# Two later head groups of dilated attention, taken by residue mod 4 with their own softmax

## The chip, the cores and the metric

One core of one Trainium2 chip. The metric is the device time of one execution in microseconds (us). TensorE is called PE, VectorE DVE, ScalarE ACT, GpSimd POOL and SyncE SP.

## What is computed

One layer of a decoder with three mixers on the same normalised input: a gated convolution, stick-breaking attention and dilated windowed softmax attention, merged by gates, then an MLP. It runs for a prompt of 512 tokens and for 8 sequences of one new token each (520 columns in all). The change is in the dilated attention of the prompt: three groups of four heads of 64 channels, with (window, dilation) of (128, 1), (512, 4) and (2048, 16). The groups' outputs are weighted by their softmax denominators, which is one softmax over the keys of all three groups:

```python
DIL_GROUPS = ((128, 1), (512, 4), (2048, 16))
...
    logits = jnp.einsum('nbqhd,nbkhd->nbhqk', qs, kb).astype(jnp.float32) * (HEAD_DIM ** -0.5) + bias
    logits = jnp.where(valid[None, :, None], logits, -jnp.inf)
    lse = jax.nn.logsumexp(logits, axis=-1)
    p = jnp.exp(logits - lse[..., None])
    o = jnp.einsum('nbhqk,nbkhd->nbqhd', p.astype(v.dtype), vb)
...
def combine_groups(outs, lses, dtype):
    w = jax.nn.softmax(jnp.stack(lses, axis=0), axis=0)
    o = jnp.sum(w[..., None] * jnp.stack(outs, axis=0).astype(jnp.float32), axis=0)
```

A query of group 1 sees only keys at a distance that is a multiple of 4, one of group 2 only multiples of 16.

## The kernel before

Every weight of the layer is streamed once, in units of 128 output channels. A unit is loaded by SP (`wraw`, three slots), split by ACT into a high part (`whi`) and by POOL or DVE into the rest (`wlo`). PE then works through **ticks**: a tick is one half (260 columns) of one unit, 24 matmuls (8 slices of the input, 3 products each: `whi` by `xh`, `whi` by `xl`, `wlo` by `xh`) into a PSUM bank of the ring G0, G1, G2. There are 324 ticks. DVE takes each result (`take`), so a bank is used again three ticks later. Units come in this order: sq, sk, sv (ticks 0 to 23), dq, dk, dv (24 to 59, six tiles each), four times cc, ch, cb (60 to 83), gates g0, g1, g2 (84 to 107), and from tick 108 the branches, out, up and down. After the second half of a `ch` tile DVE runs `convolve`, six instructions over `convu` and `convy` (ticks 63, 69, 75, 81).

Everything else is laid between the ticks by `make_plan`: a table of stages by half tick. Every engine walks the same table in order and runs its part of each stage, so an entry sets the order on all engines. A stage at an even entry stands in the middle of a tick for PE (after 12 of the 24 matmuls), one at an odd entry at the tick's end; on DVE and ACT the odd ones come after the take and after the `whi` split. Around the change stand `p_*` (stick-breaking attention of the prompt, ticks 20 to 59), `dv_rows` (transposes of dv), `v_sum` (one page step of the sampled sequences, four pages of 256 KB loaded by SP), `s_*` (dilated attention of the sampled sequences) and `branch_split` (ACT and DVE split the finished branches, `convy`, `o_sbT`, `o_dT`, into high and low parts).

The dilated attention of the prompt runs from tick 61 to tick 101. A work item w is a pair of heads `jp` (0, 1; e is the head in the pair) and a block `i` of 128 queries. Its stages: `l_scores` for each group g, queries of block i by the keys, in token order: the last 256 of them for group 0, and all keys up to the block's end for groups 1 and 2, 128 (i + 1) columns, in which `bias` masks what the dilation leaves out (by a value of -1e30). The scores go to the banks S0 (e = 0) and S1 (e = 1), one each; DVE scales them and adds the bias into `lg`, and after the third group takes the maximum over all 384 to 1280 columns (`lmax`). `l_weights`: ACT's exponential in place, with the row sum in `stat`. `l_turn`: PE transposes the blocks of one head and one group to the bank TR, ACT copies them to `lT`. `l_sum`: PE sums the values by them into the bank OU. At the end of each pair of heads `l_out` copies OU to `o_dT`, `l_root` turns the reciprocals `rsum` of the row sums, and `l_mul` spreads them over 64 rows each and multiplies. The bank TR is shared with `dv_rows`, `s_turn`, `s_vd`, `v_red` and `p_turn`; OU with `p_sum`. A bank is opened on PE by a wait until the engine that read its last contents is done. An fp32 matmul shows in the trace as two instructions.

## Time and profile before

| | |
|---|---|
| median of 3 runs | 1104.13 us (1103.65 to 1106.02) |
| the profiled execution | 1104.08 us |
| its span in the trace | 1102.3 us |
| PE busy | 1050.9 us, 95% |
| DVE, ACT, POOL busy | 41%, 38%, 28% |
| DMA | 211.08 MB, 191 GB/s on average |

The span runs from the first instruction to the last. Busy time of PE is counted from a matmul's start to its modelled end, and neighbours overlap, so 95% doesn't mean a PE at its peak: what a matmul costs is read from the distance of one start to the next. Start times in the views are microseconds from the span's start.

### The profile page before, as it was taken

What the parts mean: (1) busy time and instruction counts of PE and PEld (TensorE: products, weight loads), DVE (VectorE), ACT (ScalarE), POOL (GpSimd) and SP (SyncE); (2) the same over time, 40 slices, a digit from 0 to 9 for tenths busy, and PEclk for the clock granted to TensorE, in tenths of its full rate; (3) what the DMA queues carried; (4) which work ended last, traced back from release to release, by engine and by line L of the source; (5) the groups of instructions that cost most, each with busy time, mean ns of one, the idle gap of its engine ahead of it and who ended that gap; (6) DMA issues with size and microseconds to landing.
All of it is one profiled execution on the core that took longest, in us unless ns stands there. A gap on an engine that the chain in (4) does not pass through costs nothing.

```text
span 1102.3 us, 21957 instructions
## 1 busy us (share of the span) xinstructions
PE 1050.9 (95%) x8694; PEld 947.8 (86%) x8694; DVE 453.5 (41%) x805; ACT 422.0 (38%) x730; POOL 310.7 (28%) x141
## 2 busy tenths in 40 slices
PE   6999999998999989999999999989999999999995
PEld 6886778876778667778999999989999999999995
DVE  5313455775145523333543476743113212212434
ACT  5214556674233222334333323454134224313534
POOL 2422232211222220001212122224443444334620
PEclk9999999999999998999999999999999999999998
DMA  7588887774885575511422325736557367467202
GB/s 270 181 271 300 288 249 232 262 238 153 291 279 197 174 267 178 187 58 40 174 96 88 100 82 190 283 111 248 207 203 272 137 243 284 145 258 267 77 1 78
DMA packets 65945, 211.08 MB, mean 191 GB/s; under 512 B 7850, under 2 KB 10155, under 8 KB 63667
## 3 DMA queue, kind: packets, MB, share of 16 engines
q1 hardware_dynamic: 65842, 209.67, 55.2%
q8 instruction: 70, 1.15, 0.4%
q14 instruction: 33, 0.26, 0.1%
HBM read 202.16 MB, written 51.48 MB: 230 GB/s over the span
## 4 chain that ended last, share of the span: by engine, by line
PE 83%; DVE 5%; ACT 4%; issue 3%; DMA 2%; SPq 1%; POOL 1%; DVEq 0%; ACTq 0%
PE G L1284 52%; PE S L1284 14%; PE Z L1284 11%; PE TR L1287 3%; PE OU L1284 2%; DMA wraw<-in_w_in_dram 2%; ACT whi L681 1%; POOL wlo L653 1%; DVE convy L958 1%; SPq L543 1%; SPq L544 1%; ACT lg L824 0%; DVE mtmp L958 0%; DVE macc L955 0%; DVE pw L1149 0%
## 5 line engine op out<-in xcount | busy, mean ns | idle before, releaser
L1284 PE MATMUL G<-xh,whi 128*128 128x260 f32 x1288 | 380.3, 295 | 14.2 <-DVE xl L958 9.8
L1284 PE MATMUL G<-xl,whi 128*128 128x260 f32 x1288 | 366.8, 285 | 0.0
L1284 PE MATMUL G<-xh,wlo 128*128 128x260 f32 x1288 | 366.1, 284 | 0.0
L653 POOL TENSOR_TENSOR wlo<-wraw,whi 128x1024 fp32r<-128x1024 f32 x61 | 149.1, 2444 | 533.1 <-ACT whi L681 533.1
L1284 PEld LDWEIGHTS G<-xh,whi 128*128 128x128 f32 x1288 | 246.0, 191 | 44.2 <-issue 29.5
L1284 PEld LDWEIGHTS G<-xl,whi 128*128 128x128 f32 x1288 | 245.9, 191 | 0.0
L1284 PEld LDWEIGHTS G<-xh,wlo 128*128 128x128 f32 x1288 | 245.4, 191 | 0.0
L653 POOL TENSOR_TENSOR wlo<-mraw,whi 128x1024 fp32r<-128x1024 f32 x56 | 135.2, 2415 | 201.6 <-ACT whi L681 201.5
L681 ACT ACTIVATE whi<-wraw 128x1024 fp32r<-128x1024 f32 x83 | 87.9, 1059 | 221.8 <-PE G L1284 185.1
L681 ACT ACTIVATE whi<-mraw 128x1024 fp32r<-128x1024 f32 x56 | 59.4, 1061 | 157.3 <-PE G L1284 54.9
L955 DVE TENSOR_TENSOR tg<-G,rstd 128x260 f32<-128x260 f32 x48 | 20.4, 427 | 85.1 <-PE G L1284 85.0
L1284 PE MATMUL G<-hidh,whi 128*128 128x260 f32 x192 | 54.3, 283 | 0.0
L1284 PE MATMUL G<-hidh,wlo 128*128 128x260 f32 x192 | 54.2, 282 | 0.0
L1284 PE MATMUL G<-hidl,whi 128*128 128x260 f32 x192 | 54.1, 282 | 0.0
L1284 PE MATMUL S<-xh,whi 128*128 128x260 f32 x176 | 50.5, 287 | 2.9 <-DVE xl L955 2.9
L955 DVE TENSOR_TENSOR hT<-hT,G 128x260 f32<-128x260 f32 x47 | 19.9, 423 | 77.2 <-PE G L1284 77.2
L1284 PE MATMUL S<-xl,whi 128*128 128x260 f32 x176 | 50.2, 285 | 0.0
L1284 PE MATMUL S<-xh,wlo 128*128 128x260 f32 x176 | 50.1, 285 | 0.0
L1284 PE MATMUL G<-binh,whi 128*128 128x260 f32 x160 | 45.7, 285 | 1.3 <-issue 1.3
L955 DVE TENSOR_TENSOR hidl<-msq,hidh 128x260 fp32r<-128x260 f32 x64 | 44.7, 699 | 4.8 <-ACT hidh L681 4.8
L900 ACT ACTIVATE msq<-mt 128x260 f32<-128x260 f32 x64 | 26.5, 414 | 52.4 <-DVE mt L958 52.4
L1284 PE MATMUL G<-binh,wlo 128*128 128x260 f32 x160 | 45.2, 283 | 0.0
(261 smaller groups left out, 2090.3 us busy)
## 6 DMA issues: line engine op xcount, KB each, us to landing
wraw<-in_w_in_dram SPq DMA_DIRECT2D x66, 512.0 KB, 5.0
kv<-in_kpool_dram SPq DMA_DIRECT2D x128, 256.0 KB, 3.3
kv<-in_vpool_dram SPq DMA_DIRECT2D x128, 256.0 KB, 3.4
mraw<-in_w_up_dram SPq DMA_DIRECT2D x32, 512.0 KB, 3.5
mraw<-in_w_down_dram SPq DMA_DIRECT2D x32, 512.0 KB, 3.5
out_win_k_kept_dram<-in_cache_win_k_dram SPq DMA_DIRECT2D x8, 2047.0 KB, 9.1
out_win_v_kept_dram<-in_cache_win_v_dram SPq DMA_DIRECT2D x8, 2047.0 KB, 10.5
wraw<-in_w_ab_dram SPq DMA_DIRECT2D x8, 512.0 KB, 3.4
```

The costliest lines, as they stand in the source:

```text
L543: page = sp.value_load(pages[0:1, idx:idx + 1], min_val=0, max_val=x["kpool"].shape[0] - 1)
L544: sp.dma_start(kv[:, slot, 512 * p:512 * p + 512], x["kpool"][bass.ds(page, 1)].rearrange("a p c -> (a p) c")).then_inc(kv_in[slot], 16)
L653: nc.gpsimd.tensor_tensor(low(u), raw(u)[0], high(u).bitcast(F32), ALU.subtract).then_inc(w_lo, 1)
L681: return nc.scalar.activation(out, in_, ACT.Copy, **kw)
L900: nc.scalar.activation(msq[:, h], mt[:, h], ACT.Square).then_inc(m_sq, 1)
L955: return nc.vector.tensor_tensor(out, a, b, op)
L958: return nc.vector.scalar_tensor_tensor(out, a, scalar, b, op0, op1)
L1284: return nc.tensor.matmul(out, lhsT, rhs, start=start, stop=stop, **kw)
L1287: return nc.tensor.transpose(out, in_, ident[0:rows, 0:rows])
```

## The change

- dq, dk and dv of tiles 2 to 5 (groups 1 and 2) are stored in residue order: token 4p + r at column 128 r + p of the first 512. DVE's take writes them so, with a stride; the take of the second half becomes two instructions, since the 8 columns of the sampled tokens stay where they are. The host turns the stored dk and dv back.
- A query of residue r meets in groups 1 and 2 only keys of residue r. A step is now `(jp, sub, i)`: sub 0 is group 0, one block of queries by two blocks of keys (one for i = 0) as before; sub 1 is groups 1 and 2 together, i is the residue, and each of the two groups has one block of 128 keys. There are 16 steps (`LSTEPS`) of at most 256 columns for each head.
- The two subs have their own maximum and sum (`lstat`), their own OU contents and outputs (`o_dT`, `o_sub`). They are joined at the end: `l_stat` turns maxima and sums into rows, DVE and ACT (`l_power`) make from them a share for each sub (`share`), and `l_mul` spreads the shares, multiplies both outputs and adds them.
- `lg` is a ring of four steps instead of one item; both heads of a step are transposed in one `l_turn` of up to four blocks, and `lT` has two halves that steps use in turn. `bias` is loaded once, 1 MB, instead of four loads of 640 KB.
- One step stands at each whole tick from 61 on: scores of step m at tick 61 + m, weights a tick later, transposes two, sums three. All are odd entries. `v_sum` is rounded to the same entries. The join is at ticks 78 to 82, `branch_split` at 96 and 97 (before at 100 and 101). `s_turn` and `s_vd` move to 64 and 65.

The diff, cut; of the stage functions of DVE, ACT and PE (in this order, behind the take) only what stands there now, since the lines that they replace are printed above.

```diff
-BW = 1280
+BW = 512
 ...
-    for w in range(DLI):
-        jp, i = w // QB, w % QB
-        t = l0 + 4.5 * w + 1.5 * jp
-        if i == 0:
-            add(l0 - 3 if jp == 0 else t - 1.5, "bias_load", jp)
-        for g in range(NG):
-            add(t + 0.5 * g, "l_scores", NG * w + g)
-        add(t + 1.5, "l_weights", w)
-        for g in range(NG):
-            add(t + 2.5 + g, "l_turn", 6 * w + 2 * g)
-            add(t + 3 + g, "l_turn", 6 * w + 2 * g + 1)
-            add(t + 3.5 + g, "l_sum", NG * w + g)
-        if i == QB - 1:
-            add(t + 5.5, "l_out", jp)
-            add(t + 3.5, "l_root", jp)
-            add(t + 6, "l_mul", jp)
-    l_end = t + 6
+    add(l0 - 3, "bias_load")
+    for m in range(LSTEPS):
+        add(l0 + m, "l_scores", m)
+        add(l0 + m + 1, "l_weights", m)
+        add(l0 + m + 3, "l_sum", m)
+        if m % QB == QB - 1:
+            add(l0 + m + 3, "l_out", m // QB)
+        add(l0 + m + 2, "l_turn", m)
+    t = l0 + LSTEPS
+    add(t + 1, "l_stat", 0)
+    add(t + 2, "l_power")
+    add(t + 2, "l_stat", 1)
+    add(t + 4, "l_mul", 0)
+    add(t + 5, "l_mul", 1)
+    l_end = max(t + 6, v_end + 6, at("cb", 3) + 2)
 ...
-                    tt(plain[kind][:, tile, half(h)], src, root, ALU.mult).then_inc(dve_took, 1)
+                    if kind in ("dq", "dk", "dv") and tile >= 2:
+                        n = HALF if h == 0 else S - HALF
+                        dst = by_residue(plain[kind][:, tile, 0:S])[:, h * HALF // 4:(h * HALF + n) // 4, :]
+                        rows = [in_order(a[:, 0:n]) for a in (src, root)]
+                        if h == 0:
+                            tt(dst, *rows, ALU.mult).then_inc(dve_took, 1)
+                        else:
+                            link(tt(dst, *rows, ALU.mult))
+                            tt(plain[kind][:, tile, S:TOK], src[:, n:HALF], root[:, n:HALF], ALU.mult).then_inc(dve_took, 1)
+                    else:
+                        tt(plain[kind][:, tile, half(h)], src, root, ALU.mult).then_inc(dve_took, 1)
 ...
             def l_scores(m):
+                jp, sub, i, blocks = l_step(m)
+                n, end = P * blocks, BW if sub else 256
                 if m == 0:
                     await_bank(dve, "p_sum", QB - 1)
+                    dve.wait_ge(bias_in, 16)
+                if m >= LRING:
+                    await_bank(dve, "l_turn", m - LRING)
+                logits = lg[:, m % LRING, :, 0:n]
                 for e in range(2):
                     src = await_bank(dve, "l_scores", m, e)
+                    stt(logits[:, e, :], src[:, 0:n], SCALE, bias[:, 2 * jp + e, end - n:end],
                         ALU.mult, ALU.add).then_inc(of(read, "l_scores", m, e), 1)
+                for e in range(2):
+                    await_taken(dve, "l_scores", m, e)
+                nc.vector.tensor_reduce(lstat[:, 0, sub, i, 2 * jp:2 * jp + 2], logits, AX.X, ALU.max,
+                                        negate=True).then_inc(l_made, 1)
+            def l_stat(kind):
+                own, sub, both = share[0:GH, 0, :], share[0:GH, 1, :], share[0:GH, 0:2, :]
+                low, more = share[0:GH, 2, :], share[0:GH, 3, :]
+                srcs = [await_bank(dve, "l_stat", kind, n)[0:GH, :] for n in range(2)]
+                if kind == 0:
+                    await_bank(dve, "l_turn", LSTEPS - 1)
+                    nc.vector.tensor_copy(own, srcs[0]).then_inc(of(read, "l_stat", 0, 0), 1)
+                    nc.vector.tensor_copy(in_order(sub), by_residue(srcs[1])).then_inc(of(read, "l_stat", 0, 1), 1)
+                    for n in range(2):
+                        await_taken(dve, "l_stat", 0, n)
+                    link(tt(low, own, sub, ALU.min))
+                    tt(both, low.unsqueeze(1).to_broadcast([GH, 2, S]), both, ALU.subtract).then_inc(l_less, 1)
+                else:
+                    dve.wait_ge(l_power, 1)
+                    tt(low, srcs[0], own, ALU.mult).then_inc(of(read, "l_stat", 1, 0), 1)
+                    tt(in_order(more), by_residue(srcs[1]), in_order(sub), ALU.mult).then_inc(of(read, "l_stat", 1, 1), 1)
+                    for n in range(2):
+                        await_taken(dve, "l_stat", 1, n)
+                    link(tt(low, low, more, ALU.add))
+                    link(nc.vector.reciprocal(low, low))
+                    tt(both, both, low.unsqueeze(1).to_broadcast([GH, 2, S]), ALU.mult).then_inc(l_share_made, 1)
             def l_mul(jp):
+                parts = (o_dT[:, jp, 0:S], o_sub[:, jp, :])
+                for sub in range(2):
+                    await_taken(dve, "l_sum", 2 * jp + sub)
+                    src = await_bank(dve, "l_mul", jp, sub)
+                    tt(parts[sub], parts[sub], src[:, :], ALU.mult).then_inc(of(read, "l_mul", jp, sub), 1)
+                for sub in range(2):
+                    await_taken(dve, "l_mul", jp, sub)
+                tt(parts[0], parts[0], parts[1], ALU.add).then_inc(l_done, 1)
 ...
+            def l_weights(m):
+                jp, sub, i, blocks = l_step(m)
+                act.wait_ge(l_made, m + 1)
                 for e in range(2):
+                    col = 2 * jp + e
+                    logits = lg[:, m % LRING, e, 0:P * blocks]
+                    nc.scalar.activation(logits, logits, ACT.Exp, bias=lstat[:, 0, sub, i, col:col + 1],
+                                         accum_out=lstat[:, 1, sub, i, col:col + 1]).then_inc(l_pmade, 1)
             def l_turn(m):
+                cols = 2 * P * l_step(m)[3]
+                copy(lT[:, m % 2, 0:cols], await_bank(act, "l_turn", m)[:, 0:cols]).then_inc(read["TR"], 1)
+            def l_out(n):
+                jp, sub = n // 2, n % 2
+                src = await_bank(act, "l_sum", n)
+                if sub:
+                    copy(in_order(o_sub[:, jp, :]), by_residue(src[:, :])).then_inc(read["OU"], 1)
+                else:
+                    copy(o_dT[:, jp, 0:S], src[:, :]).then_inc(read["OU"], 1)
+            def l_powers(_):
+                act.wait_ge(l_less, 1)
+                nc.scalar.activation(share[0:GH, 0:2, :], share[0:GH, 0:2, :], ACT.Exp).then_inc(l_power, 1)
 ...
             def l_scores(m):
+                jp, sub, i, blocks = l_step(m)
                 if m == 0:
                     pe.wait_ge(dve_took, at("dk", 5) + 1)
                 dst = [open_bank(pe, "l_scores", m, e) for e in range(2)]
+                queries = slice(P * i, P * i + P)
+                keys = queries if sub else slice(P * (i + 1 - blocks), P * i + P)
+                for n in range(2 if sub else 1):
+                    for e in range(2):
+                        t, rows = head(GH * (sub + n) + 2 * jp + e)
+                        out = dst[e][:, P * n:P * n + P] if sub else dst[e][:, 0:P * blocks]
+                        ins = mm(out, dqT[rows, t, queries], dkT[rows, t, keys], True, True)
+                        if n == sub:
+                            ins.then_inc(of(written, "l_scores", m, e), 1)
+            def l_turn(m):
+                blocks = l_step(m)[3]
+                pe.wait_ge(l_pmade, 2 * m + 2)
+                dst = open_bank(pe, "l_turn", m)
                 for e in range(2):
+                    for b in range(blocks):
+                        c = P * (blocks * e + b)
+                        ins = turn(dst[:, c:c + P], lg[:, m % LRING, e, P * b:P * b + P])
                 ins.then_inc(written["TR"], 1)
             def l_sum(m):
+                jp, sub, i, blocks = l_step(m)
+                if m == 0:
+                    for n in range(2 * NG):
+                        await_taken(pe, "dv_rows", n)
+                if m % QB == 0:
+                    open_bank(pe, "l_sum", m // QB)
+                await_taken(pe, "l_turn", m)
+                for b in range(blocks):
+                    g, rows = (1 + b, i) if sub else (0, i + 1 - blocks + b)
                     for e in range(2):
                         d0 = 256 * g + HD * (2 * jp + e)
+                        c = P * (blocks * e + b)
+                        ins = mm(bank["OU"][HD * e:HD * e + HD, P * i:P * i + P], dv_tok[:, rows, d0:d0 + HD],
+                                 lT[:, m % 2, c:c + P], b == 0, b == blocks - 1, tile_position=(0, HD * e))
+                if m % QB == QB - 1:
                     ins.then_inc(written["OU"], 1)
+            def l_stat(kind):
+                if kind == 0:
+                    pe.wait_ge(l_made, LSTEPS)
+                else:
+                    pe.wait_ge(l_pmade, 2 * LSTEPS)
+                for sub in range(2):
+                    dst = open_bank(pe, "l_stat", kind, sub)
+                    for i in range(QB):
+                        ins = turn(dst[0:GH, P * i:P * i + P], lstat[:, kind, sub, i, :])
+                    ins.then_inc(of(written, "l_stat", kind, sub), 1)
             def l_mul(jp):
+                pe.wait_ge(l_share_made, 1)
+                for sub in range(2):
+                    dst = open_bank(pe, "l_mul", jp, sub)
+                    for e in range(2):
+                        col = 2 * jp + e
+                        ins = mm(dst[HD * e:HD * e + HD, :], ident[0:GH, col:col + 1].to_broadcast([GH, HD]),
+                                 share[0:GH, sub, :], True, True, tile_position=(0, HD * e))
+                    ins.then_inc(of(written, "l_mul", jp, sub), 1)
```

In what follows, `S<-dkT,dqT` are the scores, `TR<-ident,lg` transposes, `OU<-lT,dv_tok` value sums, `Z<-kv,wT` a page sum and `G<-xh,whi` the projection.

PE around tick 75, whose first half is done when the first row comes; this is before, with one group's scores in the middle of the tick and another group's at its end:

```order
L1284 MATMUL OU<-lT,dv_tok 64x128 [waits read_TR]
L1284 MATMUL OU<-lT,dv_tok 64x128 x5
L1287 MATMUL TR<-ident,lg 128x128 [waits read_TR,l_pmade]
L1287 MATMUL TR<-ident,lg 128x128 x2
L1284 MATMUL S<-dkT,dqT 128x256 [waits read_S1,read_S0]
L1284 MATMUL S<-dkT,dqT 128x256
L1284 MATMUL G<-xh,whi 128x260
```

And with the change, the end of tick 75, after 24 projection matmuls in a row:

```order
L1320 MATMUL Z<-kv,wT 32x512 [waits kv_in1]
L1320 MATMUL Z<-kv,wT 32x512 x3
L1320 MATMUL OU<-lT,dv_tok 64x128 [waits read_TR]
L1320 MATMUL OU<-lT,dv_tok 64x128 x3
L1323 MATMUL TR<-ident,lg 128x128 [waits read_TR,l_pmade]
L1323 MATMUL TR<-ident,lg 128x128 x3
L1320 MATMUL S<-dkT,dqT 128x128 [waits read_S1,read_S0]
L1320 MATMUL S<-dkT,dqT 128x128 x3
```

Each request for the score banks moves to the end of a tick, with everything else of the step ahead of it.

DVE at the same place, before: `convolve` of tick 75, then the reads of both groups' scores and two maxima.

```order
L1133 TENSOR_SCALAR convy<-convu,cvec 128x520 [waits dve_done]
L958 SCALAR_TENSOR_TENSOR convy<-convu,cvec,convy 128x512 [waits dve_done] x2
L958 SCALAR_TENSOR_TENSOR convy<-cvec,convy 128x8 [waits dve_done]
L1137 COPY utail<-convu 128x10 [waits dve_done]
L958 SCALAR_TENSOR_TENSOR convy<-cvec,convy 128x8 [waits dve_done]
L958 SCALAR_TENSOR_TENSOR lg<-S,bias 128x512 [waits written_S0,bias_in]
L958 SCALAR_TENSOR_TENSOR lg<-S,bias 128x512 [waits written_S1]
```

And with the change, DVE at tick 75 and the first rows of tick 76:

```order
L962 SCALAR_TENSOR_TENSOR convy<-cvec,convy 128x8 [waits dve_done]
L962 SCALAR_TENSOR_TENSOR lg<-S,bias 128x256 [waits written_S0,written_TR]
L962 SCALAR_TENSOR_TENSOR lg<-S,bias 128x256 [waits written_S1]
L1190 TENSOR_REDUCE lstat<-lg 128x2 [waits read_S1,read_S0]
L959 TENSOR_TENSOR convy<-convy,G 128x260 [waits made,conv_made]
```

Behind the convolution DVE now reads one step of 256 columns for each head and takes one maximum for both, then comes the next take. The join on DVE, at ticks 78 and 79 (the middle row is the take of tick 79):

```order
L1199 COPY share<-S 4x512 [waits written_TR,written_S1,written_S0]
L1200 COPY share<-S 4x512
L959 TENSOR_TENSOR share<-share 4x512 [waits read_S1,read_S0]
L959 TENSOR_TENSOR share<-share 4x1024 [waits dve_done]
L959 TENSOR_TENSOR convu<-G,rstd 128x260 [waits made]
L959 TENSOR_TENSOR share<-S,share 4x512 [waits l_power,written_S1,written_S0]
L959 TENSOR_TENSOR share<-S,share 4x512
L959 TENSOR_TENSOR share<-share 4x512 [waits read_S1,read_S0]
L1212 RECIPROCAL share<-share 4x512 [waits dve_done]
L959 TENSOR_TENSOR share<-share 4x1024 [waits dve_done]
```

It is new; the takes of ticks 79 to 81 stand between and behind its parts.

## Rows read from the trace of the kernel before

**Rows 1.** The page, engines: busy us, share of the span, instructions.
```profile
PE 1050.9 (95%) x8694; PEld 947.8 (86%) x8694; DVE 453.5 (41%) x805; ACT 422.0 (38%) x730; POOL 310.7 (28%) x141
```

**Rows 2.** Chain of waits in order of time: start us, us, what.
```profile
539.24 107.19 PE G L1284 x894
```

**Rows 3.** Busy time by stretch: stretch, its us, PE, PEld, DVE, ACT, POOL, clock, DMA share, GB/s.
```profile
289.14:524.70 235.56, 223.74 (x1805) 172.42 (x1803) 92.51 (x165) 77.55 (x137) 42.23 (x17) 0.98 0.55 184
372.00:380.00 8.00, 5.80 (x37) 3.56 (x36) 5.93 (x11) 0.41 (x1) 0.00 (x0) 0.79 0.54 161
409.00:421.00 12.00, 7.72 (x41) 5.41 (x41) 7.07 (x14) 1.31 (x4) 2.50 (x1) 0.72 0.26 89
...
296.60:302.10 5.50, 5.50 (x45) 4.17 (x44) 1.41 (x5) 1.66 (x2) 2.38 (x1) 1.00 1.00 375
```

**Rows 4.** PE's waits in 289.14:524.7: waiting <- releaser: total us, times, longest us.
```profile
PE S L1284 <- DVE lg L958: 6.5, 2, 4.3
PE TR L1287 <- ACT lT L681: 1.6, 2, 0.8
PE TR L1287 <- ACT o_dT L681: 1.2, 1, 1.2
```

**Rows 5.** Groups of PE instructions in 289.14:524.7: count | busy us, mean ns | idle before.
```profile
L1287 PE MATMUL TR<-ident,lg 128*128 128x128 f32 x108 | 21.3, 288 | 2.4 <-ACT o_dT L681 1.2 <-ACT o_sbT L681 0.6 <-ACT vd L681 0.6
L1284 PE MATMUL S<-dkT,dqT 64*128 64x256 f32 (+3 forms) x96 | 19.1, 475 | 6.5 <-DVE lg L958 6.5
L1284 PE MATMUL OU<-lT,dv_tok 128*64 128x128 f32 x216 | 17.1, 284 | 0.6 <-ACT lT L681 0.6
```

**Rows 6.** Timeline of PE, six places: start us, us, instruction, count.
```profile
336.64 0.66 PE L1284 MATMUL OU<-lT,dv_tok 128*64 128x128 f32 x8
337.23 0.44 PE L1287 MATMUL TR<-ident,lg 128*128 128x128 f32 x2
337.43 0.37 PE L1284 MATMUL G<-xh,whi 128*128 128x260 f32 x1
337.63 0.28 PE L1284 MATMUL G<-xl,whi 128*128 128x260 f32 x1
...
369.32 1.13 PE L1284 MATMUL S<-dkT,dqT 64*128 64x512 f32 x4
370.38 0.39 PE L1284 MATMUL G<-xh,whi 128*128 128x260 f32 x1
...
392.86 0.66 PE L1287 MATMUL TR<-ident,lg 128*128 128x128 f32 x4
393.28 0.37 PE L1284 MATMUL G<-xh,whi 128*128 128x260 f32 x1
...
404.64 1.07 PE L1284 MATMUL TR<-rT,ident 2*64 2x512 f32 x4
405.65 0.49 PE L1284 MATMUL S<-dkT,dqT 64*128 64x128 f32 x4
406.07 0.39 PE L1284 MATMUL G<-xh,whi 128*128 128x260 f32 x1
```

**Rows 7.** Timeline of DVE at tick 75: start us, us, instruction, count.
```profile
368.03 0.43 DVE L955 TENSOR_TENSOR convu<-convu,G 128x260 f32<-128x260 f32 x1 [0.86 <-PE G L1284]
...
369.48 3.53 DVE L958 SCALAR_TENSOR_TENSOR convy<-convu,cvec,convy 128x512 f32<-128x512 f32 x2
...
373.66 1.28 DVE L958 SCALAR_TENSOR_TENSOR lg<-S,bias 128x512 f32<-128x512 f32 x2
```

**Rows 8.** Groups of ACT and DVE by shape: count | busy us, mean ns.
```profile
L681 ACT ACTIVATE qz<-sqT 64x32 f32<-64x32 f32 x2 | 0.5, 256 | 0.0
L681 ACT ACTIVATE dvs<-dvT 128x48 f32<-128x48 f32 x1 | 0.2, 225 | 0.0
...
L1183 DVE RECIPROCAL rsum<-stat 128x8 f32<-128x8 f32 x2 | 0.4, 193 | 0.0
L1219 DVE RECIPROCAL scol<-scol 128x1 f32<-128x1 f32 x1 | 0.2, 152 | 0.0
```

**Rows 9.** PE's waits in 240:289: waiting <- releaser: total us, times, longest.
```profile
PE TR L1287 <- DVE pT L1158: 5.3, 4, 2.6
```

More of the change, by code:

```diff
@@ L1503, in l_scores @@
             def l_scores(m):
-                w, g = m // NG, m % NG
-                jp, i = w // QB, w % QB
-                full, first, _ = n_keys(i)
+                jp, sub, i, blocks = l_step(m)
                 if m == 0:
                     pe.wait_ge(dve_took, at("dk", 5) + 1)
-                k0 = full - first if g == 0 else 0
                 dst = [open_bank(pe, "l_scores", m, e) for e in range(2)]
-                for e in range(2):
-                    t, rows = head(GH * g + 2 * jp + e)
-                    mm(dst[e][:, 0:full - k0], dqT[rows, t, P * i:P * i + P], dkT[rows, t, k0:full], True,
-                       True).then_inc(of(written, "l_scores", m, e), 1)
@@ L1602, in prompt_bias @@
 def prompt_bias(rel_bias):
[L1604 to L1608 removed]
+    out = np.full((P, GH, BW), MASK, np.float32)
+    row, col = np.arange(P)[:, None], np.arange(P)[None, :]
+    near = P + row - np.arange(2 * P)[None, :]
+    for g, c, dist in ((0, 0, near), (1, 2 * P, 4 * (row - col)), (2, 3 * P, 4 * (row - col))):
+        dil = DIL[g][1]
         ok = (dist >= 0) & (dist % dil == 0) & (dist // dil <= P)
@@ L1611, in prompt_bias @@
         for j in range(GH):
-            out[j, :, col:col + width] = np.where(ok, rel_bias[b, GH * g + j], np.float32(MASK))
-        col += width
+            out[:, j, c:c + dist.shape[1]] = np.where(ok, rel_bias[b, GH * g + j], np.float32(MASK))
     return out
```

155 lines of the change are left out of this document (43 added, 112 removed).

## Prediction

> **What bounds the kernel now.** I read the page's busy line first: TensorE (PE) is busy 95% of the span, and no other engine reaches half of it [rows 1]. Then the chain of waits in order of time: late in the kernel it runs through 894 projection matmuls in a row, 107.19 us, or 0.120 us each [rows 2]. A tick is 24 of them, 2.88 us, and the kernel has 324 ticks. So time can only be gained where PE does something other than projections, where it waits, or where its clock is low. Then the stretch that the change touches, from the start of tick 60 to the start of tick 104 (289.14 to 524.70): 235.6 us for 44 ticks that alone would take 44 x 2.88 = 126.7. The other 109 us are what stands between the projections. DMA is busy 55% of it, at 184 GB/s, VectorE (DVE) 39% [rows 3], so neither is the bound on average. The last view is who PE waited for in it [rows 4]. The waits are few but dear: two of them, on DVE's `lg`, cost 6.5 us.
>
> **Matmul work removed.** The counts are 96, 108 and 216 instructions for scores, transposes and value sums [rows 5]; an fp32 matmul shows as two, so these are 24 pairs of heads for scores, 108 transposed blocks, and 24 runs of sums. Prices are the distance from one start to the next in the timeline [rows 6]. Scores of one head pair: 0.42 us for 128 keys (405.65 to 406.07), 1.06 for 512 (369.32 to 370.38); in between I draw a line, 0.63 for 256 and 0.85 for 384. Before: 6 pairs of 128 keys, 10 of 256, 4 of 384, 4 of 512: 2.5 + 6.3 + 3.4 + 4.2 = 16.4 us. After: 18 pairs of 128 and 6 of 256: 7.6 + 3.8 = 11.4. Transposes: 0.20 us for a run of 2, 0.42 for 4, so about 0.3 for 3 and 0.09 for 1. Before 12, 20, 8 and 8 runs of 1, 2, 3 and 4 blocks: 1.1 + 4.0 + 2.4 + 3.4 = 10.9; after 2 runs of 2 and 14 of 4: 6.3. Value sums: a run of 8 instructions takes 0.59 (336.64 to 337.23), a run of 12 follows the same slope; I use 0.37, 0.59, 0.81 and 1.03 for 4, 8, 12, 16. Before 6, 10, 4, 4 of these: 2.2 + 5.9 + 3.2 + 4.1 = 15.4; after 2 and 14: 9.0. The joining: before 2 runs of four small transposes (0.4) and 2 spreads over 64 rows (1.01, 404.64 to 405.65), 2.8 us; after 4 and 4 of them, 5.6. In all 45.5 before, 32.3 after: **-13.2 us**, all of it on PE and so on the path.
>
> **Fewer interruptions.** After other work, the first projection matmul lasts 0.20 instead of 0.12 us (337.43 to 337.63) [rows 6], and the last one before it is drawn out about as much: 0.16 us an interruption. By the plan, PE leaves the projection at 73 half ticks of this stretch before, and at 39 after, since a step now stands whole at a tick's end. 34 x 0.16 = **-5.4 us**.
>
> **Waits removed.** The two `lg` waits come from DVE's order. At the last tick of each `ch` tile DVE takes the bank and convolves: it begins at 368.03 and gets to `lg` at 373.66, 5.6 us later [rows 7]. The score banks S0 and S1 are single. Before, PE asks for them again half a tick later and stands; after, a whole tick later: 2.88 us of projection, a page sum (1.0), value sums (0.6) and transposes (0.4) behind the first request, and 2.0 us of the same kind before that projection. That is some 7 us against 5.6 + 1.3 for DVE. It just fits, so I let the 6.5 us go. The two waits on `lT` before `rsum` (1.6) and the one on `o_dT` (1.2) go with the code that has them [rows 4]: 9.3 in all. The clock goes with them: granted 0.79 of full over 372:380 and 0.72 over 409:421 [rows 3], the two places of the `lg` waits. At 1.2 instead of 2.4 GHz that is 3.4 and 6.7 us at half speed, half of it lost: 5.1 us. Together **-14.4 us**. What is late next is nothing on PE: the next step's scores have their bank a tick ahead.
>
> **What it adds.** (a) Takes of dq, dk and dv for tiles 2 to 5 now write with a stride of 128 elements, and those of the second half are two linked instructions. The trace has no strided DVE write. ScalarE (ACT) has one: `qz`, 32 scattered elements, 256 ns, against `dvs`, 48 in runs of 8, 225 ns [rows 8]: about 1.4 ns an element more than its own contiguous rate. From that, a take costs 0 to 0.36 us more, and 0.2 more where it is split. DVE is not PE's bound there; but four waits on `pT` (5.3 us) stand in 240:289 [rows 9], and a take lies in front of the longest. Bounds 0 and 3 us; I take 1.0. (b) The join on DVE after step 15: two copies, minimum, subtraction, then after ACT's exponential two products, a sum, a reciprocal of 4x512, a product. 8 elements of reciprocal take 193 ns and one 152 [rows 8], so 512 take some 3 us; the rest are instructions of 0.7 to 1.2 us. The chain is about 13 us from the start of tick 79, and PE wants the result at the end of tick 81, 2.9 + 2 x 4 + 2 = 13 us later. A wait of 0 to 4 us; I take 0.7. Queued behind it on DVE are takes 80 and 81, which PE needs three ticks later: hidden. (c) `branch_split` now stands at ticks 96 and 97, in ticks of 2.88 us without any cover: its 1.9, 1.9 and 1.1 us on ACT delay `whi`. It was so before too; +1.0. (d) The supply of V pages, below: +0.5. One load of the bias of 1 MB takes the place of four of 640 KB, a gain where nobody waits: nothing. Sum **+3.2 us**.
>
> At (a) the Trainium skill speaks against the change: the page SBUF — State Buffer, section Door 1: The DMA port swizzle, says in its note on cachelines that an access that crosses to a new 16-byte line pays a penalty, so fp32 may stride 4 elements for free. It gives no price. If every element paid one more DVE cycle, the 24 takes would grow by 0.27 us each; no row here shows it for DVE.
>
> **The sum.** -13.2 - 5.4 - 14.4 + 3.2 = -29.8 us. The profiled run took 1104.08 us with a span of 1102.3, and the median of the runs is 1104.13, so nothing has to be corrected: **1074 us**.
>
> **Rivals.**
> 1. *The convolution still holds the banks, or the join comes late.* The fit above is about 7 against 6.9 us. If it fails at the three ticks 63, 69 and 75 and at the join by 1 to 2 us each, PE stands 4 to 7 us and the clock falls once or twice (1.7 us each, as at 372:380): +7, 1081 us. For it: DVE's two long convolution instructions take 3.53 us [rows 7], and what feeds the steps between (ACT's exponentials) follows them. Against: DVE's own work of a step is shorter than before, two reads of 256 columns and one maximum.
> 2. *The pages become the bound.* From tick 78 on only page sums stand between the projections: 1.15 ticks at 2.88 and one sum, 4.5 us for 1.05 MB of pages and 0.30 MB of weights, 300 GB/s. In 296.60:302.10 the queues moved 375 GB/s with DMA full [rows 3], so it fits; if 285 GB/s were the limit, 0.25 us for each of 11 sums, and a wait with a drop of the clock behind it: +5, 1079 us.
> 3. *Strided takes are dear.* DVE is loaded in ticks 28 to 59. At twice the ACT surcharge, 0.7 us a take, its waits on `pT` grow and ACT is late behind it: +6 to +10, 1082 us.
> 4. *Slower than before, the same place, by another price:* 24 strided takes in 24 ticks. PE may reuse a G bank three ticks later, so a take hides until DVE itself is full. In ticks 40 to 59 DVE has about 1.2 us free a tick. Beyond that, each us of a take is a us of PE: from 2.5 us more a take (5 times 0.42, 10 ns an element) the 24 takes cost 24 x 1.3 = 31 us and the gain is gone; at 3 us it would be 24 x 1.8 = 43, 1117 us. Only if each element took ten cycles.
> 5. *It doesn't do what it says:* the stretch is not bound by PE. Its 95% and the 13.2 us of matmul speak against; 1104 us.
>
> **How the numbers follow.** The forecast (1068 to 1079) has 0.60, rivals 1 and 2 together 0.20 (1077 to 1087), rival 3 0.09, rival 4 0.03, rival 5 0.02. In 0.06 it is better than 1068: all added costs hidden, 1104.1 - 33.0 = 1071, and the short waits on `vd`, `o_sbT` and `lT` that I left uncounted gone too. The range 1066 to 1086 leaves out rivals 4 and 5, the dear end of rivals 1 and 3, and what lies beyond 1066: 0.16. Faster by over 0.2% (2.2 us, about what a measurement of this kernel can tell): 0.95; within 0.2%: 0.02; slower: 0.03.
>
> **What would show it.** In the profile after: S<-dkT, TR<-ident,lg and OU<-lT with 96, 60 and 120 instructions; ticks 61 to 77 of about 5.7 us each; no wait of PE for `lg` over 1 us and a granted clock of 1.00 from tick 61 to tick 104; the stretch of ticks 60 to 103 at 204 to 207 us. Takes `dqT<-G` with shape 65x4 at 0.42 to 0.8 us. Wrong: PE waits for `lg` at ticks 64, 70, 76; `kv` pages among PE's releasers; takes over 1 us.

## The result, and the profile after

The changed kernel takes **1071.55 us** (median of 4 runs, 1069.96 to 1073.68), the kernel before 1103.98 (1103.65 to 1106.02). The ratio is 0.971, with a 95% interval of 0.967 to 0.974: 32.4 us less, where 1074 us and 30 us less were forecast. The profiled run took 1069.96 us with a span of 1067.9.

The page of after, busy us of each engine; beside [rows 1] PE gives up 23 us (its weight loads, PEld, 13), and no other engine moves by more than 10:

```profile
PE 1027.5 (96%) x8566; PEld 934.8 (88%) x8566; DVE 458.4 (43%) x812; ACT 412.2 (39%) x731; POOL 311.2 (29%) x141
```

Busy time by stretch (stretch, its us, PE, PEld, DVE, ACT, POOL, clock, DMA share, GB/s): first ticks 60 to 103, which answer to 289.14:524.70 in [rows 3], then the place of the join:

```profile
287.65:490.38 202.73, 200.45 (x1676) 160.10 (x1675) 92.71 (x162) 68.06 (x139) 42.16 (x17) 1.00 0.62 203
...
400.00:418.00 18.00, 16.54 (x117) 10.60 (x116) 16.23 (x23) 2.00 (x2) 2.37 (x1) 1.00 0.68 209
```

The stretch fell from 235.6 to 202.7 us, by 32.8, and the clock is 1.00 all through it. DMA moves 203 instead of 184 GB/s. All of PE's waits in it, beside [rows 4]:

```profile
PE S L1320 <- DVE o_dT L959: 0.9, 1, 0.9
PE G L1320 <- POOL wlo L651: 0.8, 1, 0.8
PE S L1320 <- DVE share L959: 0.5, 1, 0.5
```

No wait for `lg` is left. Two short ones for the join are new. The groups that answer to [rows 5] (count | busy us, mean ns | idle before):

```profile
L1320 PE MATMUL OU<-lT,dv_tok 128*64 128x128 f32 x120 | 10.1, 286 | 0.0
L1323 PE MATMUL TR<-ident,lg 128*128 128x128 f32 x60 | 10.1, 288 | 0.0
L1320 PE MATMUL S<-dkT,dqT 64*128 64x128 f32 x72 | 6.7, 300 | 0.0
L1320 PE MATMUL S<-dkT,dqT 64*128 64x256 f32 x24 | 4.2, 428 | 0.0
```

Last, the block of other work at the end of tick 75, in PE's timeline (start us, us, instruction, count), and the start of the next block:

```profile
372.14 1.06 PE L1320 MATMUL Z<-kv,wT 128*32 128x512 f32 x8
373.14 0.66 PE L1320 MATMUL OU<-lT,dv_tok 128*64 128x128 f32 x8
373.73 0.66 PE L1323 MATMUL TR<-ident,lg 128*128 128x128 f32 x4
374.31 0.71 PE L1320 MATMUL S<-dkT,dqT 64*128 64x128 f32 x8
374.96 0.39 PE L1320 MATMUL G<-xh,whi 128*128 128x260 f32 x1
...
378.04 0.64 PE L1320 MATMUL Z<-kv,wT 128*32 128x512 f32 x4
```

A whole tick with a page sum and a softmax step is 378.04 - 372.14 = 5.90 us. Read the starts, not the durations, since those overlap: 1.00 for the page, 0.59 for value sums, 0.58 for transposes, 0.65 for scores, 3.08 for the projection. The prediction had 5.7. In what follows I add up such distances over ticks 60 to 103, each given to the instruction that starts it. Each column adds up to its stretch. A wait is in the instruction ahead of it, and the last row says how much of the column is waits.

```
us, ticks 60 to 103      before   e2      e1      after   e12
scores                    17.4    16.5     9.8     9.8     9.8
transposes of lg          13.7    13.7     5.7     8.7     6.2
value sums                17.7    15.4     9.0     9.0     9.0
joining                    2.7     2.7     5.3     5.3     5.3
projections              147.8   141.1   137.1   135.4   136.1
pages and the rest        36.2    35.3    36.5    34.6    33.7
stretch                  235.5   224.7   203.4   202.7   200.2
of it waits               11.9     5.4     3.2     2.2     1.3
```

Columns e2, e1 and e12 are experiments, below. Of the waits, 6.9, 2.6, 0.8, 1.3 and 1.3 us lie in the row of the projections, and 1.6 in that of the transposes before and in e2 (the two on `lT`).

### The profile page after: what moved, and what is told of

Same layout as the page of the kernel before. It is cut to its first block, busy times and chain, and to the rows that moved or that the text cites. A ratio compares the mean times of both kernels' runs of the same rounds, so it can differ in the third digit from the quotient of the medians.

```text
span 1067.9 us, 21643 instructions
## 1 busy us (share of the span) xinstructions
PE 1027.5 (96%) x8566; PEld 934.8 (88%) x8566; DVE 458.4 (43%) x812; ACT 412.2 (39%) x731; POOL 311.2 (29%) x141
## 4 chain that ended last, share of the span: by engine, by line
PE 87%; DVE 5%; ACT 3%; issue 2%; DMA 1%; POOL 1%; SPq 0%; DVEq 0%; ACTq 0%
PE G L1320 56%; PE S L1320 14%; PE Z L1320 12%; PE TR L1323 2%; PE OU L1320 2%; DMA wraw<-in_w_in_dram 1%; ACT whi L679 1%; POOL wlo L651 1%; DVE mtmp L962 0%; DVE macc L959 0%; DVE pw L1164 0%; DVE pT L1173 0%; DVE convu L959 0%; DVE share L1212 0%; PE TR L1320 0%
## 5 line engine op out<-in xcount | busy, mean ns | idle before, releaser
L1320 PE MATMUL G<-xh,whi 128*128 128x260 f32 x1288 | 375.5, 292 | 12.7 <-DVE xl L962 9.7
```

Of the source, the lines that this page charges most:

```text
L1320: return nc.tensor.matmul(out, lhsT, rhs, start=start, stop=stop, **kw)
```

## Experiments

### The waits alone

**e2_scores_first** is the kernel before, with the convolution moved behind the scores:

```
 elif kind == "ch":
     ...
-    if h:
-        convolve(tile)
 ...
+if k and TICKS[k - 1][1][0] == "ch" and TICKS[k - 1][2]:
+    convolve(TICKS[k - 1][1][4])
 take(k)
```

> The kernel before, with one edit on VectorE: the convolution of a tile runs after the read of the scores that PE sends in the next half ticks, instead of ahead of it. Matmul work and plan are as before. Theory: the two waits on lg (6.5 us) and the two falls of the clock behind them (5.1 us) go, 1104 - 11.6 = 1092.5 us (1091 to 1095), and the granted clock in 372:380 and 409:421 is 1.00. Rival A, the clock falls for another reason than the waits: only 6.5 us, 1097.5. Rival B, VectorE is late by as much somewhere else (a G bank, lT): 1102 to 1105.

Measured: 1092.85 us (1092.22 to 1094.93). Its stretch of ticks 60 to 103, and the two places at which the clock was 0.79 and 0.72 in [rows 3]:

```profile
287.39:512.14 224.75, 219.37 (x1804) 169.78 (x1803) 90.23 (x165) 77.56 (x137) 41.97 (x17) 1.00 0.58 193
372.00:380.00 8.00, 8.00 (x68) 6.42 (x66) 7.44 (x12) 4.18 (x6) 0.84 (x1) 1.00 0.70 212
405.00:421.00 16.00, 16.00 (x129) 12.14 (x128) 7.94 (x19) 6.78 (x14) 1.34 (x2) 1.00 0.74 233
```

DVE in it, at the same scores as [rows 7]:

```profile
368.84 1.29 DVE L958 SCALAR_TENSOR_TENSOR lg<-S,bias 128x512 f32<-128x512 f32 x2 [1.66 <-PE S L1284]
372.31 1.29 DVE L958 SCALAR_TENSOR_TENSOR lg<-S,bias 128x512 f32<-128x512 f32 x2 [2.19 <-PE S L1284]
...
376.82 1.54 DVE L958 SCALAR_TENSOR_TENSOR convy<-convu,cvec,convy 128x512 f32<-128x512 f32 x2
```

Now DVE waits for the scores, and PE no longer waits for DVE. With no matmul removed the stretch is 10.8 us shorter, where the theory gives 11.6 (6.5 of waits, 5.1 of clock). Rivals A (only the waits) and B (the wait moves) fall. The edit alone makes the kernel before 1% faster, and one third of the whole gain was two waits and what the clock made of them.

### Half ticks against whole ticks

**e1_half_ticks** is the kernel after with its work spread over both halves of a tick:

```
-        t = int(v0 + 1.15 * i + 1.5 * (i // PAGES))
+        t = v0 + 1.15 * i + 1.5 * (i // PAGES)
 ...
-        add(l0 + m + 3, "l_sum", m)
+        add(l0 + m + 4, "l_sum", m)
-        add(l0 + m + 2, "l_turn", m)
+        add(l0 + m + 2.5, "l_turn", m)
```

(`l_out` and the join follow a tick later.)

> The kernel after, with the same instructions spread over both halves of a tick: transposes a half tick later, value sums and the join a whole tick later, page sums at the half ticks they had before. Between the start of tick 60 and that of tick 104, PE then leaves the projection 55 times instead of 39. Theory, an interruption costs 0.16 us: the stretch grows from 202.7 by 2.6 us, to 205.3. Rival A, an interruption costs nothing on PE and only waits do: under 203.2. Rival B, the half tick between transposes and value sums is too short or DVE is asked too soon: waits of over 1 us, 206 or more.

Measured: 1071.27 us (1067.47 to 1075.32). The stretch, and its waits:

```profile
283.72:487.12 203.40, 200.09 (x1676) 160.29 (x1675) 92.37 (x162) 68.60 (x139) 42.25 (x17) 1.00 0.63 206
```

```profile
PE TR L1323 <- ACT spself L679: 1.0, 1, 1.0
PE S L1320 <- DVE share L959: 0.9, 1, 0.9
PE G L1320 <- POOL wlo L651: 0.8, 1, 0.8
PE TR L1323 <- ACT vd L679: 0.6, 1, 0.6
```

The stretch is 0.7 us longer than after's. It waits 3.2 us where after waits 2.2; without waits it is 200.2 against 200.5. So 16 more interruptions cost nothing in sum. That is rival A in substance, though its bound of 203.2 is missed by 0.2. But the table shows that an interruption has a price: without their waits the projections grow from 134.1 to 136.3 us, 0.14 for each of the 16. What makes up for it is that the transposes shrink by 3.0 us with the same 60 instructions. The transposes in e1's timeline, alone in the middle of a tick:

```profile
372.62 0.60 PE L1323 MATMUL TR<-ident,lg 128*128 128x128 f32 x4
372.98 0.37 PE L1320 MATMUL G<-xh,whi 128*128 128x260 f32 x1
```

Four transposes take 0.36 us here and 0.58 between value sums and scores. So their price depends on what stands beside them.

**e12_turns_last** tests that with the number of interruptions left at 39: the order inside the block becomes value sums, scores, transposes.

```
 for m in range(LSTEPS):
+    add(l0 + m + 3, "l_sum", m)
+    ...
+for m in range(LSTEPS):
     add(l0 + m, "l_scores", m)
+for m in range(LSTEPS):
     add(l0 + m + 1, "l_weights", m)
-    add(l0 + m + 3, "l_sum", m)
-    ...
     add(l0 + m + 2, "l_turn", m)
```

> The kernel after, with the order inside the block at the end of a tick changed on PE: value sums, scores, transposes, in place of value sums, transposes, scores. The count of interruptions stays at 39. Theory now: not leaving the projection has a price, but a change of kind between the small matmuls; a run of four transposes takes 0.587 us ahead of scores and 0.414 ahead of the projection, so the 15 ticks win 0.17 us each: -2.6 us in the stretch (202.7 to 200.1). Rival, the order is indifferent, and the first turn to another kind always costs the same: 202.7. Second rival, the scores ask for their banks 0.6 us sooner, behind the convolution of ticks 63, 69 and 75: a wait for lg of up to 0.5 us each.

Measured: 1069.97 us (1066.71 to 1070.82), against 1070.06 for after on the same chip. The medians can't tell 2.5 us apart, as the runs of one kernel lie 4 to 7 us apart there. The stretch can:

```profile
287.93:488.16 200.23, 198.88 (x1675) 160.75 (x1675) 92.62 (x162) 68.17 (x139) 42.16 (x17) 0.99 0.62 206
```

```profile
372.22 0.66 PE L1325 MATMUL TR<-ident,lg 128*128 128x128 f32 x4
372.63 0.37 PE L1322 MATMUL G<-xh,whi 128*128 128x260 f32 x1
```

200.2 us, 2.5 less than after, where 2.6 was expected; four transposes take 0.41 us, all of them together 2.5 us less, and there is no wait for `lg`. Both rivals fall. But two things that the expectation didn't have are in the 2.5. The granted clock fell to its lower level in the stretch, ahead of the last products of the join:

```profile
405.70:409.10 3.40, 3.40 (x19) 3.00 (x21) 3.19 (x8) 0.00 (x0) 0.00 (x0) 0.50 0.38 145
```

The matmuls there lose 1.6 us, and PE comes so late to the join that its wait of 0.9 us on `o_dT` in after is gone. That is 0.7 us net on the wrong side, so the agreement with 2.6 is partly luck, and at a level clock the order should be worth more than 2.5.

The block still changes its kind of matmul as often as in after. What has changed is the neighbour of the transposes, and by it the distances in the timelines fall into order. Transposes and projections use all 128 rows and columns of PE, page sums 32 columns, value sums 64 columns and scores 64 rows. Four transposes take 0.36 us between projections, 0.41 between a matmul of the smaller kinds and a projection, and 0.58 or 0.59 between a smaller one and scores. Page sums (1.00) and eight value sums (0.59) take the same whatever stands beside them. So it is the step from the transposes to smaller matmuls that costs, 0.17 us, and not each change of kind. The distances in before, e2, e1, after, e9 and e12 all fit this; it was read from them and not tested apart, and why it costs, no run shows.

**after_again** is the kernel after, run beside e12, e4 and e11:

> The kernel after, unchanged, to stand beside the other three on the same chip: 1071.5 us (1069.5 to 1074). By the trace, runs differ from each other only before tick 24 and in a fall of the clock near 250 us and 690 us.

Measured: 1070.06 us (1066.89 to 1073.48), ticks 60 to 103 in 202.6 us and ticks 24 to 59 in 186.08, against 202.7 and 186.06. Between these two runs such a stretch repeats within 0.1 us, with the clock up in both, and this is why stretches decide where medians don't.

### Is it PE's work that counts?

**e3_work_twice** issues every score matmul and every transpose twice:

```
-for n in range(2 if sub else 1):
+for n in (0, 1, 0, 1) if sub else (0, 0):
 ...
-for e in range(2):
+for e in (0, 1, 0, 1):
     for b in range(blocks):
         ...
         ins = turn(
```

> The kernel after, with every score matmul and every transpose of the later head groups issued twice into the same place; the result is the same. Theory, PE bounds the stretch, so work counts one for one: scores 2 x 0.42 + 6 x 0.63 + 8 x 0.645 = 9.8 us, transposes 6.3 us by the prediction's prices, +16.1 us on the kernel after (1071.5): 1087.6 (1085 to 1090). Rival, PE has slack in the stretch that the waits of other engines fill: +0 to +8, under 1080.

Measured: 1082.6 us (1080.66 to 1084.56). The stretch:

```profile
287.21:502.89 215.68, 213.40 (x1831) 172.78 (x1831) 92.74 (x162) 68.04 (x139) 42.05 (x17) 1.00 0.59 191
```

It grew by 13.0 us instead of 16.1, with the same waits as after; the median grew by 11.1 and lies below the range that was expected. That isn't slack. Added up from the timeline, the second run of eight scores takes 0.446 us instead of 0.645, of four transposes 0.436 instead of 0.587, of two pairs of 256 keys 0.431: 8 x 0.446 + 6 x 0.431 + 2 x 0.22 + 14 x 0.436 + 2 x 0.22 = 13.1. So work counts one for one, at the price of a run right behind its like. The size in the expectation was off, the mechanism is right.

### The strided takes

**e4_plain_takes** leaves out the reordering by residue (the edit makes `if kind in ("dq", "dk", "dv") and tile >= 2:` false).

> The kernel after with the takes of dq, dk and dv for tiles 2 to 5 written without the stride of 128 and in one instruction, so that the later head groups are computed on tokens in the wrong order; every instruction after the takes is as before. The prediction gave the strided takes +1.0 us (0 to 3): the kernel would be 1.0 us faster than after_again, all of it in ticks 24 to 59. Rival, a take is hidden behind the three ticks until its bank is asked for again: 0.0 to 0.2 us in ticks 24 to 59.

Measured: 1068.9 us (1065.38 to 1072.43) against 1070.06. The takes of dk, first in after, then in e4 (groups of DVE: count | busy us, mean ns):

```profile
L959 DVE TENSOR_TENSOR dkT<-G,rstd 128x260 f32<-128x260 f32 x8 | 4.2, 519 | 0.0
L959 DVE TENSOR_TENSOR dkT<-G,rstd 128x252 f32<-128x252 f32 x4 | 2.5, 616 | 0.0
L959 DVE TENSOR_TENSOR dkT<-G,rstd 128x8 f32<-128x8 f32 x4 | 0.7, 167 | 0.1
```

```profile
L959 DVE TENSOR_TENSOR dkT<-G,rstd 128x260 f32<-128x260 f32 x12 | 5.0, 420 | 0.0
```

Of the first group half are strided: 2 x 519 - 420 = 0.62 us against 0.42, so 0.20 more for 260 elements, and 0.36 more for the half that is two instructions. On PE nothing of it arrives: ticks 24 to 47 take 115.45 us in e4 and 115.46 in after_again. In ticks 48 to 53 e4 is even 1.3 us slower, because the clock fell at PE's longest wait on `pT` (2.6 us):

```profile
249.00:258.00 9.00, 6.57 (x40) 5.38 (x40) 5.12 (x11) 4.10 (x7) 1.92 (x1) 0.81 0.05 6
```

The profile of after has the same wait (2.8 us) without the fall, so this is one of the things that make runs of one kernel differ. The medians, 1.2 us apart, lie within the scatter of either kernel. The rival holds: 0.0 and not 1.0 us.

**e5_takes_3x** and **e6_takes_5x** issue the strided product three and five times (a loop of two and of four more around `link(tt(dst, *rows, ALU.mult))`).

> The kernel after, with the strided product in each of the 24 takes of dq, dk and dv for tiles 2 to 5 issued three times on VectorE: +1.24 us a take. Theory (rival 4 of the prediction): VectorE has about 1.2 us free a tick in ticks 40 to 59, so this hides but for the waits on pT: +0 to +4 us on 1071.5. Rival, VectorE is already on the path there and each us counts: 24 x 1.24 = +30, 1101.

> The kernel after, with the strided product of each of the 24 takes issued five times: +2.48 us a take. Theory (rival 4 of the prediction, 2.5 us more a take): VectorE is full from 1.2 us on, (2.48 - 1.2) x 24 = +31 us on 1071.5, 1102 (1092 to 1112), as slow as the kernel before. Rival, a take hides up to three ticks and VectorE catches up between: under +10, 1081.

Measured: 1073.71 (1071.79 to 1077.99) and 1087.04 us (1086.07 to 1089.36). Ticks 24 to 59, which take 186.1 us in after, first in e5, then in e6, and what PE waits for in e6:

```profile
98.99:289.99 191.00, 181.19 (x1591) 142.52 (x1591) 142.39 (x239) 108.16 (x219) 46.21 (x19) 0.98 0.74 237
```

```profile
101.09:304.70 203.61, 180.88 (x1592) 142.61 (x1591) 166.10 (x285) 108.42 (x219) 45.87 (x19) 0.98 0.68 222
```

```profile
PE TR L1325 <- DVE pT L1175: 16.2, 8, 5.3
PE OU L1322 <- DVE pT L1175: 5.2, 6, 2.0
```

After's DVE is busy 111.2 us there. With 31 us more in e5 PE loses 4.9 us, part of it to the clock; the median grew by 2.2, inside the 0 to 4 that were expected. With 55 us more in e6 (60 were reckoned) it loses 17.5. The expectation for e6 was 31, so the 1.2 us a tick that DVE was said to have free were too few. Both expectations for e6 missed. The mechanism of rival 4 exists, as waits on `pT`, and lies where it was sought, at about half of its price.

### How tight the fit is

**e8_conv_longer** issues the first product of a convolution seven times (`for _ in range(7):`).

> The kernel after, with the first product of each of the four convolutions issued seven times on VectorE instead of once: +2.9 us a tile. Theory, the fit of the prediction's rival 1 is tight: by the trace of after VectorE frees a score bank about 1.0 us ahead of PE's request, so PE waits 1.9 us for lg after ticks 63, 69 and 75 and 2.9 us longer for the join, +8.6 us, and the granted clock falls at one or more of these places: 1080 to 1087. Rival, the score banks come free long before: only the join is late, +3, 1074.5.

Measured: 1083.9 us (1082.54 to 1088.75). PE's waits in ticks 60 to 103:

```profile
PE S L1321 <- DVE lg L962: 5.7, 3, 2.3
PE S L1321 <- DVE o_dT L959: 2.6, 1, 2.6
```

And the clock at two of the four places, behind tick 69 and at the join:

```profile
346.50:355.70 9.20, 7.52 (x50) 5.48 (x50) 6.81 (x18) 1.48 (x5) 0.00 (x0) 0.81 0.80 276
...
413.70:430.30 16.60, 13.98 (x75) 10.01 (x75) 13.39 (x24) 0.68 (x1) 2.36 (x1) 0.79 0.48 144
```

The waits are back, 2.3 us behind tick 63 and 1.7 behind 69 and 75. By DVE's timeline the read of the scores ends 3.2 us later than in after. So the kernel after has some 0.9 us to spare at the first of the three ticks and 1.5 at the other two; its own timeline, from the end of that read to PE's next scores, gives the same. That is the size of the prediction's "it just fits". The 2.9 us that the expectation reckoned with became 3.2 by two changes that nearly cancel, told at the end under DVE and POOL.

### Better versions

**e9_turns_apart** takes away waits that are left in after:

```
-            add(at("dv", 2 * g + 1) + 1.5 + r, "dv_rows", 2 * g + r)
+            add(at("dv", 2 * g + 1) + 2 + r, "dv_rows", 2 * g + r)
-        add(at("sv", 3) + 1 + 0.5 * i, "sv_rows", i)
+        add(at("sv", 3) + 1 + i, "sv_rows", i)
-    add(t + 4, "l_mul", 0)
-    add(t + 5, "l_mul", 1)
+    add(t + 5, "l_mul", 0)
+    add(t + 6, "l_mul", 1)
```

> The kernel after, with three of its remaining waits taken away by the plan: the transposes of the dv rows stand half a tick later and those of the sv rows a tick apart, so that they do not ask for bank TR right beside the transpose of a softmax step, and the last products of the join stand one tick later. Theory: the waits on pT (5.4 us), on sv_tok (1.2) and of the join (0.9 and 0.5) go, -8.0 us: 1063.5 (1062 to 1066). Rival, VectorE or ScalarE is late there as such, and the waits move to the next softmax steps: 1069 to 1072.

Measured: **1061.95 us** (1060.93 to 1062.84), a ratio to before of 0.962 (0.959 to 0.965). Ticks 24 to 59 fell from 186.1 to 180.0, and PE's only waits over 0.4 us between tick 24 and tick 104 are these two (ticks 24 to 59, then 60 to 103):

```profile
PE TR L1323 <- DVE pT L1173: 1.3, 1, 1.3
```

```profile
281.08:481.87 200.79, 199.98 (x1675) 159.81 (x1675) 92.65 (x162) 67.95 (x139) 42.17 (x17) 1.00 0.62 208
```

(the other is the 0.8 on `wlo`, as in after). Two kinds of transposes had stood side by side and asked for the one bank TR; for the dv rows half a tick between them is enough, the sv rows were set a whole tick apart. The expectation was -8.0 us; the spans differ by 7.8 (1060.1 against 1067.9).

**e10_scores_half** adds `add(t + 0.5, "p_scores", n)` for `add(t, "p_scores", n)` to e9.

> As e9_turns_apart, and the 18 score steps of the first head groups stand half a tick later, in the half tick in which the transposes stand anyway: in ticks 20 to 59 PE leaves the projection 57 times instead of 67. Theory: 10 x 0.14 us less than e9_turns_apart, -1.4 us. Rival, ScalarE gets the scores 1.4 us later and is late with the weights of every other step: PE waits for pw, +2 us or more against e9_turns_apart.

Measured: 1071.79 us (1069.41 to 1072.79), 9.8 more than e9. Its waits in ticks 24 to 59:

```profile
PE OU L1320 <- DVE pT L1173: 2.5, 1, 2.5
PE TR L1323 <- DVE pT L1173: 2.5, 2, 2.0
```

The rival holds in size: ten interruptions fewer bring less than what half a tick less for the chain from scores to transposes costs. It had named `pw`, but that makes only 1.3 us of waits; most are on `pT`. Ticks 24 to 59 take 8.2 us more than in e9, and part of that is the clock, which fell behind one of the waits on `pT`. It fell in ticks 60 to 103 as well, where PE waits for nothing but `wlo` much later, and e9 has the same plan and keeps 1.00:

```profile
411.00:417.00 6.00, 6.00 (x38) 4.63 (x33) 4.88 (x11) 0.41 (x1) 0.00 (x0) 0.72 0.66 204
```

**e11_turns_alone** is e9 with the transposes in half ticks of their own (`l_turn` at `l0 + m + 2.5`, `l_sum` at `l0 + m + 4`, `s_turn`, `s_vd` and the join later).

> e9_turns_apart with the transposes of the later head groups in the first half of a tick, alone, and the value sums one tick later; s_turn and s_vd stand in the second half, out of their way. PE leaves the projection 50 times in the stretch. Theory: a run of four transposes between projections takes 0.355 instead of 0.587 us and the projection 0.08 more, so 15 ticks win 0.15 us each: -2.3 us against e9_turns_apart, 1059.7. Rival, by the prediction's 0.16 us an interruption: +1.8 us, 1063.7.

Measured: 1061.74 us (1059.03 to 1064.15), the same as e9 (on another chip), and its stretch is 200.79 us, as e9's. The transposes do shrink, from 8.7 to 5.2 us. But the clock falls at 409:416, where one tick's projection takes 4.6 instead of 3.1 us:

```profile
409.00:416.00 7.00, 7.00 (x40) 4.63 (x39) 3.55 (x6) 1.79 (x2) 0.00 (x0) 0.78 0.90 289
```

PE waits for nothing there, and why the clock falls is open. Inconclusive as a version; as to interruptions it speaks as e1 does: 14 more than in e9 cost nothing in sum, even with some 1.5 us lost to the clock. e9 with the order of e12 wasn't tried.

## Why the prediction was right

**Matmul work, -13.2: right, a little too small.** Between e2 and after, which differ in this but not in waits for `lg`, the first four rows of the table fall from 48.3 to 32.8 us. The 1.6 us of waits on `lT` are in them, which the prediction counted with the waits; the work fell by 13.9 (forecast 45.5 to 32.3). Scores give 6.7 instead of 5.0: I priced each of two pairs of a step at 0.42, but the second behind the first adds 0.22, and the two take 0.645. Value sums give 6.4 (forecast 6.4), the joining costs 2.6 (2.8). The transposes give only 3.4 (4.6), since I took 0.42 for four where after pays 0.58. So the sum is near partly because two errors, on scores and on transposes, have opposite signs.

**Fewer interruptions, -5.4: the step that stands only by half.** Without their waits the projections of after take 4.4 us less than e2's, 0.13 for each of the 34 interruptions, near the 0.16 of the prediction. Yet e1 puts 16 interruptions back and loses nothing but 1.0 us of waits. What the prediction left out is that the same move puts the transposes ahead of the scores: what a whole tick saves on the projection (2.2 us for the 16) it pays on the transposes (3.0). For those 16 my price gives 2.6 us; 0.7 came, all of it waits. From before to e1 the count also falls, from 73 to 55, but there the smaller attention has fewer pieces to place, and no run parts the two. In the sum the step did no harm: work and interruptions together, with the short waits and the costs in the stretch, were forecast at -19.2, and e2 to after measures -22.0.

**Waits and clock, -14.4: right.** e2 measures 10.8 for the part on `lg`, of 11.6. The other 2.8 (two on `lT`, one on `o_dT`) are gone from the list of waits, and so are 1.8 us of short ones that the prediction left uncounted. The clock is 1.00 in the stretch, as foretold, and e8 shows that it falls when the waits come back.

**Added costs, +3.2: 1.4 instead.** (a) Takes: 0.0, not 1.0. The cover that I named holds for the 0.20 to 0.36 us that a take costs; with 1.24 us more PE loses 4.9 us (e5). The note on cachelines in the Trainium skill (SBUF — State Buffer, Door 1: The DMA port swizzle) says that a stride beyond a line has a price, and the trace agrees: 0.62 instead of 0.42 us for 260 elements, 0.20 more, where the prediction's estimate by one more cycle each was 0.27. It is off PE's path. (b) The join: 0.5 + 0.9 = 1.4 us for the 0.7 taken, inside 0 to 4. The reciprocal of 4x512 took 3.34 us, where 3 was estimated:

```profile
398.29 1.28 DVE L959 TENSOR_TENSOR share<-S,share 4x512 f32<-4x512 f32 x2 [2.44 <-ACT share L840]
...
400.38 3.34 DVE L1212 RECIPROCAL share<-share 4x512 f32<-4x512 f32 x1
```

(c) `branch_split`: one wait of 0.8 on `wlo`, and before had that wait too; 0, not 1.0. (d) Pages: no wait on `kv`; 0, not 0.5.

**Sum.** In the stretch -30.8 was forecast (the sum of -29.8 holds 1.0 for the takes, which lie ahead of it), and -32.8 came: waits and clock 15.4, work 13.9, projections 4.4, pages and the rest 0.5 (all without waits), less 1.4 for the new waits of the join. From e2, e1 and after: 10.8 for waits and clock, 21.3 for the smaller attention with its fewer pieces, 0.7 for whole ticks. Outside the stretch +1.0 was forecast, and the medians give +0.4 (32.4 against 32.8).

**The rivals.** Rival 1: the convolution does not hold the banks, but with only 0.9 to 1.5 us to spare (e8). Rival 2: pages are not the bound; PE never waits for `kv` in the stretch. Rivals 3 and 4: a take's price is 0.2 to 0.36 us, not 0.7 or 2.5, and at 2.48 it would have cost 17.5 us (e6), not 31. Rival 5: PE does bound it (e3).

## What to carry to other kernels

Separate a wait from the work around it by letting the waiting engine's partner do its other work later: here an edit of four lines to the kernel before earned 10 of the 32 us. When small matmuls of several kinds stand together, try their order as well as the number of times that the main loop is left: here it was worth 2.5 us to put the full-size transposes ahead of the projection and not of the scores, and 16 blocks fewer were worth nothing. And when two steps share one bank, see whether they ask for it side by side: moving such steps apart brought 6 us in ticks 24 to 59 (e9).

## What the hardware showed that I had not expected

**What a transpose costs depends on its neighbours.** Four transposes of 128x128 fp32 take 0.36 us between projections, 0.41 behind scores and ahead of the projection, 0.58 between value sums (two 64-column halves) and scores (64 rows); a second run right behind the first takes 0.44. Eight value sums take 0.59 ahead of transposes, of scores and of the projection alike.

**DVE's long fp32 pair takes 3.53 or 1.54 us, by when POOL works.** The two convolution passes of [rows 7], in after, at ticks 75 and 81, and POOL's nearest splits:

```profile
373.77 3.53 DVE L962 SCALAR_TENSOR_TENSOR convy<-convu,cvec,convy 128x512 f32<-128x512 f32 x2
408.95 1.54 DVE L962 SCALAR_TENSOR_TENSOR convy<-convu,cvec,convy 128x512 f32<-128x512 f32 x2
```

```profile
373.45 2.52 POOL L651 TENSOR_TENSOR wlo<-wraw,whi 128x1024 fp32r<-128x1024 f32 x1 [8.40 <-ACT whi L679]
...
405.73 2.37 POOL L651 TENSOR_TENSOR wlo<-wraw,whi 128x1024 fp32r<-128x1024 f32 x1 [7.12 <-ACT whi L679]
```

Where POOL's split begins 0.3 us ahead of the pair, it takes 3.5 us, in all seven such cases of before and after; in the one where no split runs beside it, 1.54. In the kernel before, that is 2 us of the 5.6 for which the convolution held the score banks. e8 bears it out, though made for something else: there the pair runs when the split is over and takes 1.54 at all four tiles, and at three of them the seven first products meet the split instead:

```profile
341.97 5.64 DVE L1149 TENSOR_SCALAR convy<-convu,cvec 128x520 f32<-128x520 f32 x7
```

At the fourth tile, where they don't meet it, the seven take 3.64 us. So 2 us are lost by whichever of these DVE instructions meets the split.

**The clock falls without a wait too**, near the join: in e11 (0.78 over 409:416) and e10 (0.72 over 411:417) PE had waited for nothing, and in e12 and e4 only 0.5 us (for the join). Each time it is at the lower level for 3.4 us. In e11 a tick of projections alone stood ahead of it, then a page sum and the products of the join. The kernels after and e9, with the same plan as e4 and e10 there, keep 1.00. No run here tells why.
